# Chunk products split over three engines, r times k beside the memory attention, shifts inside the first level

## The reference, cut to what matters

```
p_tm = p_tm + (token_shift(p_tm) - p_tm) * a_shift_mu[i]
r, k, v, d_lo, a_lo, g_lo = jnp.split(p_tm, RWKV_SPLITS, axis=-1)
...
k = k * (1.0 + (lr - 1.0) * a_k_a[i])
y = rwkv7_scan(rh, heads(decay, RWKV_HEADS), kh, vh, -kk, kk * lrh)
y = head_group_norm(y, a_lnx_g[i], a_lnx_b[i])
y = y + jnp.sum(rh * kh * a_r_k[i], axis=-1, keepdims=True) * vh
y_mix = y.reshape(bsz, s_len, RWKV_DIM) * gate
m = memory_attention(heads(q_mem, MEM_HEADS), mem_n, a_mem_kv[i])
```

## Time and profile before

| What | us |
|---|---|
| median of 3 runs | 1156.02 (1154.36 to 1156.06) |
| the profiled execution | 1156.42 |
| its span in the trace | 1155.1 |
| TensorE busy in the span | 1117.1 (97%) |
| VectorE busy | 732.8 (63%) |
| ScalarE busy | 569.0 (49%) |
| GpSimd busy | 73.4 (6%) |

### The profile page before, as it was taken

One profiled execution on the slowest core, in us unless ns is written; L12 is line 12 of the kernel. 1 busy time (PEld: TensorE's weight loads), 2 busy tenths in 40 slices (PEclk: granted clock), 3 DMA queues, 4 the chain that ended last, 5 costly groups with the idle time before them and its releaser, 6 DMA issues.

```text
span 1155.1 us, 22499 instructions
## 1 busy us (share of the span) xinstructions
PE 1117.1 (97%) x9837; PEld 1063.4 (92%) x9837; DVE 732.8 (63%) x1042; ACT 569.0 (49%) x767; POOL 73.4 (6%) x134
## 2 busy tenths in 40 slices
PE   8999999999999999999799999999999999999998
PEld 8888889789999999988688999999987889999998
DVE  5557657455665556767988756555577875655553
ACT  6355646344544444684344634434365774443343
POOL 2410111100000000400000000000002000000000
PEclk9999999999999999998999999999999999999999
DMA  7933444325455554533000445555554224555551
GB/s 263 311 145 125 162 166 172 142 90 186 183 190 189 186 183 182 198 125 136 12 3 3 162 180 184 187 184 192 188 198 151 105 76 181 185 185 186 188 189 55
DMA packets 29862, 182.70 MB, mean 158 GB/s; under 512 B 3591, under 2 KB 6872, under 8 KB 8900
## 3 DMA queue, kind: packets, MB, share of 16 engines
q1 hardware_dynamic: 24608, 174.07, 41.8%
q0 software_dynamic: 1888, 4.75, 1.5%
q10 hardware_dynamic: 3268, 2.43, 0.7%
HBM read 180.18 MB, written 1.07 MB: 157 GB/s over the span
## 4 chain that ended last, share of the span: by engine, by line
PE 82%; DVE 7%; ACT 5%; issue 3%; POOL 2%; DMA 1%; ACTq 0%; DVEq 0%; POOLq 0%
PE bank L683 79%; ACT w_hi L2329 2%; DVE w_lo L1503 1%; DMA w_raw<-in_weights 1%; PE bank L697 1%; PE bank L880 1%; ACT exps L2441 1%; DVE inverse L2219 1%; DVE inverse_t L2244 0%; POOL inverse_rms_diagonals L2872 0%; DMA bias_rows<-bias_lines 0%; PE bank L687 0%; DVE chunk_products L2199 0%; PE bank L1225 0%; ACTq L2516 0%
## 5 line engine op out<-in xcount | busy, mean ns | idle before, releaser
L1503 DVE TENSOR_TENSOR w_lo<-w_raw,w_hi 128x2048 fp32r<-128x2048 f32 x157 | 358.0, 2291 | 200.1 <-ACT w_hi L2329 199.8
L2329 ACT ACTIVATE w_hi<-w_raw 128x2048 fp32r<-128x2048 f32 x161 | 306.5, 1913 | 111.4 <-DMA w_raw<-in_weights 106.2
L683 PE MATMUL bank<-x_channels_hi,w_hi 128*128 128x256 f32 x1424 | 230.8, 286 | 3.8 <-DVE proj L1575 1.3
L683 PE MATMUL bank<-x_channels_lo,w_hi 128*128 128x256 f32 x1424 | 228.3, 284 | 0.0
L683 PE MATMUL bank<-x_channels_hi,w_lo 128*128 128x256 f32 x1424 | 220.8, 278 | 0.0
L683 PEld LDWEIGHTS bank<-x_channels_hi,w_hi 128*128 128x128 f32 x1424 | 196.2, 192 | 7.6 <-issue 3.9
L683 PEld LDWEIGHTS bank<-x_channels_lo,w_hi 128*128 128x128 f32 x1424 | 194.2, 191 | 0.1
L683 PEld LDWEIGHTS bank<-x_channels_hi,w_lo 128*128 128x128 f32 x1424 | 191.7, 189 | 0.0
L683 PE MATMUL bank<-hidden_hi,w_lo 128*128 128x256 f32 x528 | 103.6, 284 | 0.0
L683 PE MATMUL bank<-hidden_hi,w_hi 128*128 128x256 f32 x528 | 102.0, 281 | 0.0
L683 PE MATMUL bank<-hidden_lo,w_hi 128*128 128x256 f32 x528 | 101.7, 280 | 0.0
(11 more groups left out here) (450 smaller groups left out, 1550.1 us busy)
## 6 DMA issues: line engine op xcount, KB each, us to landing
w_raw<-in_weights SPq DMA_DIRECT2D x163, 1024.0 KB, 4.8
mem_rows<-in_mem POOLq DMA_DIRECT2D x2, 1024.0 KB, 6.1
xn<-in_x SPq DMA_DIRECT2D x1, 1024.0 KB, 5.5
w_raw<-in_weights SPq DMA_DIRECT2D x2, 512.0 KB, 8.6
bias<-bias_rows ACTq DMA_DIRECT2D x2, 512.0 KB, 9.1
bias<-bias_rows ACTq DMA_DIRECT2D x1, 1024.0 KB, 11.0
out<-xn SPq DMA_DIRECT2D x4, 256.0 KB, 2.5
wide_masks<-in_triangle_masks POOLq DMA_DIRECT2D x1, 832.0 KB, 8.3
```

The source lines that it names most:

```text
L683: return nc.tensor.matmul(out, lhs, rhs, start=start, stop=stop)
L1503: V.tensor_tensor(k.w_lo[:, s, :], k.w_raw[:, s, :], k.w_hi[:, s, :].bitcast(F32), ALU.subtract).then_inc(k.lo_done, 1)
L2329: A.activation(k.w_hi[:, s, :], k.w_raw[:, s, :], ACT.Copy).then_inc(k.hi_done, 1)
```

## The change

Six edits:

1. VectorE's `masked` takes only the removal half of a bank (columns 0 to 63 of each chunk) with one mask.
2. ScalarE copies the query half out of the bank unmasked (`query_products`), after VectorE's half, and signals `g_a`; TensorE waits for `g_a` where it waited for `g_v`. GpSimd later multiplies the query half by its mask in place, in three instructions (6, 3 and 3 heads; 1536, 768 and 768 elements a partition), and TensorE waits for all three (`cut`) before `y` of chunk 0.
3. VectorE makes the queries and r times k at step 1 of the attention; `r_k` lies in another place in SBUF, which the first masks overwrite, so mask 0 waits for the `same_head` products.
4. TensorE makes the three `same_head` products at step 4 of the attention, into banks 0, 4 and 5, before the last head's product with the values; all chunk products wait for ScalarE's copies of them.
5. The raw pairs of `ain5` come between the two halves of the masks on VectorE, `keep_pair(5, n)` between copies 5 and 6 of the query parts on ScalarE.
6. The shifts come behind the `step` of chain 1 in level 1.

```diff
 # TensorE
+        if i == 4:
+            PE.wait_ge(*k.dve_once.at("rk", 0))
+            PE.wait_ge(*k.exped.all("m0"))
+            for n in range(3):
+                matmul(bank[RK_BANK[n]]..., k.same_head[:, :], k.rk[:, 2 * n:2 * n + 2, :], True,
+                       True).then_inc(k.pe_once.sem, 1)
     attention("m0", beside_m0)
...
+    PE.wait_ge(*k.dve_once.all("r"))
+    PE.wait_ge(*k.act_once.all("rk"))
     for h in range(0, RW_HEADS, 2):
...
         if h >= 4:
-            PE.wait_ge(*k.g_v.at("heads", h - 3))
+            PE.wait_ge(*k.g_a.at("heads", h - 3))
...
         elif piece == "y":
+            if n == 0:
+                PE.wait_ge(*k.pool_once.all("cut"))
 # VectorE, beside_m0, i == 1
+            V.wait_ge(*k.shifted.at("sh", SHIFTED.index(5)))
+            V.wait_ge(*k.dve.so_far())
+            for half in range(2):
+                V.tensor_tensor(queries(half), of_chunks(rB, half), decays(k.down, half, 1), ALU.mult)...
             for b in range(RWB):
                 r = V.scalar_tensor_tensor(out=k.rk[:, b, :], ...
...
     def masked(h):
         V.wait_ge(*k.g_p.at("heads", h))
-        V.tensor_tensor(k.g[h][:, :, :], bank[4 + h % 4]...,
-                        k.masks[:, 0:2, :]..., ALU.mult).then_inc(k.g_v.sem, 1)
+        if h == 0:
+            V.wait_ge(*k.pe_once.all("rk"))
+        V.tensor_tensor(k.g[h][:, :, 0:C], bank[4 + h % 4]...[:, :, 0:C],
+                        k.masks[:, 0:1, :].to_broadcast((P, NC, C)), ALU.mult).then_inc(k.g_v.sem, 1)
...
         turn(half)
-    shift_pair(5, 0)
-    shift_pair(5, 1)
+        if half == 0:
+            raw_pair(5, 0)
+            raw_pair(5, 1)
...
+            if (n, level) == (1, 1):
+                shift_pair(5, 0)
+                shift_pair(5, 1)
 # ScalarE
+    def query_products(heads):
+        for h in heads:
+            A.wait_ge(*k.g_v.at("heads", h))
+            A.activation(k.g[h][:, :, C:2 * C], bank[4 + h % 4]...[:, :, C:2 * C],
+                         ACT.Copy).then_inc(k.g_a.sem, 1)
+    attention("m0")
     for n in range(3):   # copies of the same_head products
...
+    query_products(range(6))
+    keep_pair(5, 0)
+    keep_pair(5, 1)
+    query_products(range(6, RW_HEADS))
 # GpSimd, behind the memsets of chunk_starts
+    for first, n, g in k.g_places:
+        G.wait_ge(*k.g_a.at("heads", first + n - 1))
+        queries = g[:, :, :, C:2 * C].rearrange("p n c t -> p (n c) t")
+        G.tensor_tensor(queries, queries, k.masks[:, 1:2, :].to_broadcast((P, n * NC, C)), ALU.mult)...
```

More of the change, by code:

```diff
@@ L315, in rw_signals @@
         self.pe_once = Signal(nc, "pe_products", mixcols=1, cols=1, up=12, squares=1, gate=3, norms=3, rk=3)
-        self.pool_once = Signal(nc, "pool_made", ident=1, half=1, ones=2, blocks=1, less=2, sig0=1, reset=1, causal=1, k_rot=2)
+        self.pool_once = Signal(nc, "pool_made", ident=1, half=1, ones=2, blocks=1, less=2, sig0=1, reset=1, cut=3, causal=1, k_rot=2)
         self.act_once = Signal(nc, "act_made", table=2, lam=1, tanh=2, ups=12, squares=1, factor=1, sqrt=1, gate=3, e1=1, e2=1, rk=3,
@@ L1326, in beside_m0 @@
             PE.wait_ge(*k.raw_made.at("ain", 7))
+        if i == 4:
+            PE.wait_ge(*k.dve_once.at("rk", 0))
+            PE.wait_ge(*k.exped.all("m0"))
+            for n in range(3):
+                matmul(bank[RK_BANK[n]][:, :].rearrange("p (k t) -> p k t", k=2), k.same_head[:, :], k.rk[:, 2 * n:2 * n + 2, :], True,
+                       True).then_inc(k.pe_once.sem, 1)
     attention("m0", beside_m0)
@@ L1348, in recurrence_tensor @@
                     m.then_inc(k.g_p.sem, 1)
-    PE.wait_ge(*k.act_once.all("rk"))
+    PE.wait_ge(*k.raw_made.all("ain"))
     PE.wait_ge(*k.o.all("m0"))
@@ L1376, in recurrence_tensor @@
             if n < 2:
-                PE.wait_ge(*k.g_v.all("heads"))
+                PE.wait_ge(*k.g_a.all("heads"))
             else:
@@ L1385, in recurrence_tensor @@
         elif piece == "keys":
-            PE.wait_ge(*(k.kb_a.at("chunk", 2 * n - 1) if n else k.g_v.all("heads")))
+            PE.wait_ge(*(k.kb_a.at("chunk", 2 * n - 1) if n else k.g_a.all("heads")))
             for j, blocks in enumerate(((0, 1, 2, 3), (4, 5))):
@@ L2176, in beside_m0 @@
                             k.up[:, :, 1:NC, 0:1].rearrange("p b c o -> p b (c o)"), ALU.mult).then_inc(k.dve_once.sem, 1)
[L2177 to L2184, removed]
+            V.wait_ge(*k.shifted.at("sh", SHIFTED.index(5)))
+            V.wait_ge(*k.dve.so_far())
+            for half in range(2):
+                V.tensor_tensor(queries(half), of_chunks(rB, half), decays(k.down, half, 1), ALU.mult).then_inc(k.dve_once.sem, 1)
             for b in range(RWB):
@@ L2198, in masked @@
         V.wait_ge(*k.g_p.at("heads", h))
-        V.tensor_tensor(k.g[h][:, :, :], bank[4 + h % 4][:, :].rearrange("p (c z) -> p c z", c=NC),
-                        k.masks[:, 0:2, :].rearrange("p a t -> p (a t)").unsqueeze(1).to_broadcast((P, NC, 2 * C)),
-                        ALU.mult).then_inc(k.g_v.sem, 1)
+        if h == 0:
+            V.wait_ge(*k.pe_once.all("rk"))
+        V.tensor_tensor(k.g[h][:, :, 0:C], bank[4 + h % 4][:, :].rearrange("p (c z) -> p c z", c=NC)[:, :, 0:C],
+                        k.masks[:, 0:1, :].to_broadcast((P, NC, C)), ALU.mult).then_inc(k.g_v.sem, 1)
     def first_inverse(n):
@@ L2779, in recurrence_scalar @@
     product("ain5", 1)
[L2781 to L2784, removed]
+    def query_products(heads):
+        for h in heads:
+            A.wait_ge(*k.g_v.at("heads", h))
+            A.activation(k.g[h][:, :, C:2 * C], bank[4 + h % 4][:, :].rearrange("p (c z) -> p c z", c=NC)[:, :, C:2 * C],
+                         ACT.Copy).then_inc(k.g_a.sem, 1)
+    attention("m0")
     split["end"] = k.total_units
```

8 lines of the change are left out of this document (6 added, 2 removed).

## The result

| | before | changed |
|---|---|---|
| median | 1155.71 us (4 runs, 1154.36 to 1156.06) | 1165.89 us (4 runs, 1164.62 to 1166.67) |
| ratio | | 1.0089, 95% interval 1.0072 to 1.0107 |
| the profiled execution | 1156.42 us, span 1155.1 | 1165.77 us, span 1164.5 |

The change makes the kernel 10 us slower. The direction and one main mechanism, GpSimd's hold on VectorE, were as forecast. The forecast of 1163.3 us was 2.6 us too low, and the measured time lies just above its range.

What follows compares the result with a forecast made beforehand. It took VectorE's stretch before the recurrence's first level, on which TensorE waits, as the bound. Terms 2.0 + 3.3 + 0.15 + 1.9 = +7.3 us gave 1163.7, median 1163.3; range 1156.6 to 1165.2.

Steps and rivals of the forecast that it cites:

- Half masks, and ScalarE in the ring: Chunk products: narrower masks at 0.37 us, banks wait for ScalarE's copies; six masks keep 0.6 of 1.6 saved, +0.4 in all.
- Masks on GpSimd: First inverses: GpSimd's masks block VectorE's two-SBUF-operand instructions for their full length, +3.3, +0.15 and +1.9 us.
- rival 1: VectorE never waits for GpSimd, only the new round trips count: 1158.0 us, from 1156.8 to 1159.0; chance 0.35.
- Residual pair between the halves: Before pair 5: keeps wait for raw pairs, copies 6 and 7 for keeps, TensorE idles; sum to +1.4 us.
- Shifts inside the first level: Level 1: nothing hides the shifts behind chain 1's step; next first_inverse at 572.9 for 570.92, sum to +2.0 us.
- Queries and r times k beside the attention: Attention: VectorE's idle 3.85 us before the maximum hides this work but for some 0.25 us; uncovered it would cost 4.2.
- forecast +2.4: Start of the last mem_v product, near 554.55 instead of 552.14, behind the same_head products.
- The clock: Pair 5 and the next product at TensorE's lower level: 1.16 and 0.92 us more at most, none taken.
- Rival 3: GpSimd blocks VectorE and TensorE's clock falls on pair 5: 1163.3 + 2.1 = 1165.4 us; chance 0.04.
- Sum: Whole run: 1156.42 us profiled plus 7.3 gives 1163.7, against a forecast median of 1163.3 us.
- the forecast stretches of the table: Forecast growth of lateness between fixed points, from the last mem_v product to the end; zero from level 2 on.

Runs made afterwards that it cites:

- e1: The changed kernel, but GpSimd's three masks wait for VectorE's last y_rest instruction in level 3 of the recurrence: 1161.69 us, ratio 1.0055.
- e6: The kernel before with edits 1 and 2 alone, GpSimd's masks as soon as their heads are copied: 1155.69 us, ratio 1.0012.
- e7: The kernel before with edits 1 and 2 alone, GpSimd's masks held back until VectorE's rest is through: 1152.06 us, ratio 0.9983.
- e2: The changed kernel with GpSimd's masks late and the raw pairs and keep_pair back beside the attention: 1160.46 us, ratio 1.0043.
- e9: The changed kernel plus unused identity products in TensorE's holes: 18 in the attention, 54 before pair 5, 26 in level 1, 28 before level 2: 1161.79 us, 1.0068.
- e5: The kernel before with edits 1 and 2, GpSimd's masks late, the same_head products behind all chunk products: 1153.82 us, ratio 0.9991.
- e10: The changed kernel with GpSimd's masks late, raw pairs and keeps back in the attention, shifts back before level 1: 1156.62 us, ratio 1.002.
- e12: The kernel before, edits 1 and 2, GpSimd's masks late, same_head products last, r times k moved into VectorE's holes: 1151.03 us, ratio 0.9978.

## Why the prediction was near, and where it failed

**Half masks, and ScalarE in the ring.** Right: six masks in 3.2 us (557.54 to 560.72) with a gap before the fifth, 0.38 to 0.40 each for 0.37, saving 0.63 for 0.6.

**Masks on GpSimd.** The mechanism is right and rival 1 is wrong: e1 and e6 against e7 show it. The size was off by 1.2: 1536 elements take 3.09 us and not 3.4, so +2.8 and +1.3 for the +3.3 and +1.9 forecast. The Trainium skill (SBUF — State Buffer, section "SBUF: two separate sides") had told this side: the pair of ports has one holder for a whole instruction, the other engine is blocked, and among those who ask for it is VectorE with two SBUF inputs while GpSimd reads SBUF. The traces agree: 3.97 against 1.14, pieces of 0.64 to 0.79 that cost 0.84, and 0.56 unchanged beside 6.31 us of GpSimd where one operand comes from PSUM.

**Residual pair between the halves.** Right in kind: ScalarE idle 5.40 before `shifted`, TensorE 6.48 before pair 5. By e1 to e2 it costs 1.4, where the forecast's running sum grew by 1.0 at this step (from +0.4 to +1.4); the intervals of e1 and e2 overlap.

**Shifts inside the first level.** The step up to the next `first_inverse` was right (3.65 from the turn; e2 shows 3.77). "I carry whatever the first level is late to the end" is what failed behind it: 2.29 us more were lost in level 2, all to the clock, since e9 loses none there.

**Queries and r times k beside the attention.** This step failed: "the hole hides them but for some 0.25 us". The hole of 3.85 stood in one execution in which TensorE had run at the lower level from 157 to 160 and from 525 to 533, and brought its logits at 545.22. With the clock up they come at 541.6, and the hole is 2.09 (e5) for 4.2 us of work. The changed kernel pays 2.1 us there, TensorE idles 2.69, and the products behind it run at the lower level: the last `mem_v` product comes 13.80 behind the logits for 6.92. With the clock held up in e9 it comes 10.83 behind them, so of the 6.88 some 3.0 are the clock's and 3.9 the order's. In the difference of the two profiles only +3.22 is left of this 6.88, because the logits of the changed run came 3.66 earlier. That the forecast +2.4 looks near is luck; e10, in which it and the `same_head` products are all that is left beside the split masks, still loses 2.3 us.

**The clock.** The failed term: "1.16 and 0.92 more at most, of which I take none". Measured by e9 it is 6.25 us from the logits on, in three places: 2.5 up to the first `first_inverse`, nearly all in the attention, 1.5 at pair 5 and level 1, and 2.3 in level 2; the forecast had none of them. It was bounded by the two products next to the hole, although in before itself the lower level had followed the hole of 3.04. Rival 3 was the right case, and its price of 2.1 was too small.

**Sum.** Of the 2.07 us between 1163.7 and the profiled 1165.77, 1.1 arose up to the next `first_inverse` (the forecast stretches of the table add up to 7.3, which puts it at 578.22; it came at 579.35: the attention +0.8, pair 5 and the product behind the second turn at the lower level +1.5, the shorter blocks -1.2), 2.29 in level 2, and -1.32 is most likely luck behind it. So the step that failed, in the forecast's own terms, is the zero taken for the clock, and with it the hole that was to hide the queries and r times k.

## What to carry to other kernels

Work handed to GpSimd with operands in SBUF belongs where VectorE reads PSUM (0.56 us unchanged here), or in short pieces: what is left of the GpSimd instruction in progress is added to a VectorE instruction with two SBUF operands that meets it. Before work is moved into a hole, ask whether that hole is there in every execution; here it was made by a slow stretch of TensorE ahead of it. And a hole added on TensorE can cost the products behind it at half the clock besides itself, here into the second level of the recurrence (2.82 for 1.97), so count these before a round trip is added to a chain of small products.

## What was not expected of the hardware

Executions of one kernel differ by where TensorE's clock falls. With the same code up to the logits, e6 ran at the lower level from 157 to 160 and from 525 to 532 and had its logits at 545.10; e7 did neither and had them at 541.62. The runs of before made beside e5 lie between 1151.9 us (mean clock 0.996) and 1160.2 (0.990), the runs of e12 between 1149.2 (0.998) and 1157.3 (0.990): on this kernel the spread is larger than most of the effects sought.

Once fallen, the clock stayed down for 24 us in the changed kernel while TensorE was busy for 13.44 of them. Useless products in the holes of the changed kernel made it faster in the trace, not slower: behind 54 of them pair 5 still waited 0.45 us for ScalarE.
